# A gated attention and convolution block: the causal branch placed second, two more gate buffers, three rows of w_out and the post norm loaded during the last tiles

## The reference, cut to what matters

```python
h = rmsnorm(x, pre_norm_w[layer], NORM_EPS)                    # (2048, 1024)
proj = h @ w_in[layer]
(q, k, v, z_att, gb, gc, u, z_conv, g_att, g_conv) = jnp.split(proj, split_idx, axis=-1)
...
att = diff_attention(q, k, v, positions, lam)     # 4 heads, each the difference of two softmaxes
att = rmsnorm(att, subln_w[layer], SUBLN_EPS) * (1.0 - lambda_init)
att = att.reshape(b, s, ATT_WIDTH) * jax.nn.silu(z_att)
y_att = att @ w_att_out[layer]
cv = gb * short_conv(gc * u, conv_w[layer])
y_conv = (cv * jax.nn.silu(z_conv)) @ w_conv_out[layer]
m = (jax.nn.sigmoid(g_att + merge_bias[layer, 0]) * y_att
     + jax.nn.sigmoid(g_conv + merge_bias[layer, 1]) * y_conv)
x = x + rmsnorm(m @ w_out[layer], post_norm_w[layer], NORM_EPS)
```

## Time and profile before

| | us |
|---|---|
| median of 3 runs | 1817.24 (1812.0 to 1818.17) |
| profiled execution | 1817.06 |
| its span, first to last instruction | 1815.3 |
| PE busy in it | 1759.0 |
| DVE busy | 893.9 |
| ACT busy | 581.3 |

### The profile page before, as it was taken

How to read it: one execution, slowest core, us unless ns; L and a number is a source line. 1 busy time by engine, 2 the same in 40 slices (tenths; PEclk the granted TensorE clock), 3 DMA queues, 4 the chain that set the end, 5 groups by cost and what they waited for, 6 DMA issues and landing times.

```text
span 1815.3 us, 22423 instructions
## 1 busy us (share of the span) xinstructions
PE 1759.0 (97%) x8512; PEld 1467.5 (81%) x8512; DVE 893.9 (49%) x1903; ACT 581.3 (32%) x1039; POOL 89.2 (5%) x74
## 2 busy tenths in 40 slices
PE   6999999999999999999999999999999989999998
PEld 5878888888888888788887888888788768888887
DVE  5537225354433611267766666766666434424252
ACT  5422112121201111244444444444444333313231
POOL 0000000000000000111101112111001000000000
PEclk9999999999999999999999999999999999999999
DMA  6438536556503446976575678656756775453532
GB/s 220 141 135 329 193 133 209 186 186 196 174 24 113 153 120 158 285 219 192 186 196 184 202 218 271 212 177 209 237 167 171 234 280 172 116 184 107 179 105 75
DMA packets 149574, 328.90 MB, mean 181 GB/s; under 512 B 14801, under 2 KB 68049, under 8 KB 135889
## 3 DMA queue, kind: packets, MB, share of 16 engines
q1 hardware_dynamic: 149458, 327.37, 57.1%
HBM read 216.16 MB, written 111.16 MB: 180 GB/s over the span
## 4 chain that ended last, share of the span: by engine, by line
PE 86%; DMA 4%; ACT 3%; SPq 3%; DVE 2%; issue 2%; DVEq 0%; ACTq 0%
PE bank L935 19%; PE bank L936 19%; PE bank L937 19%; PE bank L1059 15%; PE bank L1021 5%; PE bank L993 3%; PE bank L994 3%; PE bank L1004 2%; SPq L667 2%; ACT e L1261 2%; DMA ring<-gate_s 1%; DMA w<-split_s 1%; PE bank L945 1%; DMA gate_s<-gate_st 1%; DVE at_lo L1609 1%
## 5 line engine op out<-in xcount | busy, mean ns | idle before, releaser
L935 PE MATMUL bank<-ht,w 128*128 128x512 f32 x896 | 349.4, 390 | 2.6 <-issue 2.6
L936 PE MATMUL bank<-ht,w 128*128 128x512 f32 x896 | 349.2, 390 | 0.0
L937 PE MATMUL bank<-ht,w 128*128 128x512 f32 x896 | 349.1, 390 | 0.0
L1059 PE MATMUL bank<-ht,w 128*128 128x512 f32 x912 | 238.8, 396 | 4.2 <-DMA w<-split_s 4.2
L935 PEld LDWEIGHTS bank<-ht,w 128*128 128x128 f32 x896 | 168.5, 188 | 38.0 <-ACT w L1173 3.0
L1059 PEld LDWEIGHTS bank<-ht,w 128*128 128x128 f32 x912 | 167.3, 190 | 37.0 <-DMA w<-split_s 4.8
L937 PEld LDWEIGHTS bank<-ht,w 128*128 128x128 f32 x896 | 168.7, 188 | 35.0
L936 PEld LDWEIGHTS bank<-ht,w 128*128 128x128 f32 x896 | 168.6, 188 | 35.0
L1573 DVE CUSTOM_DVE_ANT_0 e<-bank,zeros 128x512 f32<-128x512 f32 x192 | 125.0, 688 | 129.4 <-PE bank L994 128.9
L1261 ACT ACTIVATE e<-e,nbias 128x128 f32<-128x128 f32 (+15 forms) x128 | 152.9, 1198 | 74.8 <-DVE nbias L1582 74.6
L1059 PE MATMUL bank<-hx,w 128*128 128x512 f32 x576 | 157.2, 401 | 5.7 <-DMA w<-split_s 5.7
(11 more groups left out here) (140 smaller groups left out, 2497.0 us busy)
## 6 DMA issues: line engine op xcount, KB each, us to landing
w<-split_s SPq DMA_DIRECT2D x62, 1024.0 KB, 5.4
split_s<-piece SPq DMA_DIRECT2D x24, 1024.0 KB, 4.9
q_st<-qk_s SPq DMA_DIRECT2D x128, 128.0 KB, 5.6
gate_s<-gate_st SPq DMA_DIRECT2D x64, 256.0 KB, 6.0
ring<-gate_s SPq DMA_DIRECT2D x64, 256.0 KB, 3.4
raw<-in_w_in SPq DMA_DIRECT2D x28, 512.0 KB, 5.6
ht_s<-ht SPq DMA_DIRECT2D x3, 4096.0 KB, 27.5
qk_s<-stage SPq DMA_DIRECT2D x48, 192.0 KB
```

What stands on the lines that cost most here:

```text
L935: nc.tensor.matmul(out, left[0], right[0], start=start, stop=False)
L936: nc.tensor.matmul(out, left[0], right[1], start=False, stop=False)
L937: return nc.tensor.matmul(out, left[1], right[0], start=False, stop=stop)
L1059: mm = nc.tensor.matmul(bank[2 + u % 2][:], unit_weights(u)[:, term // 2, k, :], h_slot(bb, k)[:, term % 2, :], start=i == 0, stop=i == PE ...
```

## The change

The non-causal plan becomes the body of the `If` and the causal one that of the `Else`. Ring buffers 2 and 3 change places in SBUF with `wo_hi[0]`, `br[2]` and `br[3]`, and SP loads them at the end of `attend`, right behind 0 and 1; in the causal plan without a further wait. `wo_raw[4]`, `[5]`, `[7]` and `post_w` are loaded in round 61, behind `wa[3]`. The w_out rows are loaded and split in the order 4, 5, 7, 0, 1, 2, 3, 6, from m = 1 on. The other loads of the merge's first block (`wa[5]` to `wa[7]`, `wo_raw`) take new places between ring loads 5 to 15.

```diff
-WO_AT = ((), (), (0,), (1,), (2,), (3,), (4, 5), (6, 7))
+WO_AT = ((), (4,), (5,), (7,), (0,), (1,), (2,), (3, 6))
+WO_ORDER = (4, 5, 7, 0, 1, 2, 3, 6)
+WO_KEPT = 3
...
         for k in (4, 5, 6):
             late_br(k)
+        late_wo_hi(0)
+        late_br(2)
+        late_br(3)
         late_ring(2)
         late_ring(3)
-        late_br(2)
-        late_br(3)
-        late_wo_hi(0)
         late_wo_lo(0)
...
-            with eng.If(causal == 1):
+            with eng.If(causal == 0):
+                attend(Plan(False))
+            with eng.Else():
                 attend(Plan(True))
-            with eng.Else():
-                attend(Plan(False))
...
+            def load_wo(k):
+                i = WO_ORDER.index(k)
+                sp.dma_start(wo_raw[k][:], t["w_out"][k * P:(k + 1) * P, :]
+                             ).then_inc(wo_kept if i < WO_KEPT else wo_in[i - WO_KEPT], 16)
...
                                 load_branch(0, 2)
                                 load_branch(0, 3)
                                 load_wa(3)
+                                for k in WO_ORDER[:WO_KEPT]:
+                                    load_wo(k)
+                                sp.dma_start(post_w[:], t["post_norm_w"].to_broadcast([P, D])).then_inc(post_in, 16)
...
-                ring_load(0, 0)
-                ring_load(0, 1)
+                for i in range(2):
+                    ring_load(0, i)
+
+                if not plan.causal:
+                    sp.wait_ge(pv_done, PAIRS)
+                for i in range(2, 4):
+                    ring_load(0, i)
...
             sp.wait_ge(pv_done, PAIRS)
-            for i in range(2, RING):
-                ring_load(0, i)
+            ring_load(0, 4)
             sp.wait_ge(unit_done, UNITS)
...
             load_wa(4)
+            load_wa(5)
             for s_ in att_stored:
                 sp.wait_ge(s_, 16 * PAIRS // 2)
-            load_wo(0)
-            load_wo(1)
-            load_wa(5)
...
             for i in range(RING, 2 * KT):
                 ring_load(0, i)
-                if i == RING:
-                    load_wa(6)
-                    load_wo(2)
-                    load_wo(3)
-                elif i == RING + 1:
-                    load_wa(7)
-                elif i < RING + 6:
-                    load_wo(i - RING + 2)
-                elif i == RING + 7:
-                    sp.dma_start(post_w[:], t["post_norm_w"].to_broadcast([P, D])).then_inc(post_in, 16)
+                if i in (6, 9):
+                    load_wa(6 if i == 6 else 7)
+                elif i in (7, 8, 10, 12, 13):
+                    load_wo(WO_ORDER[WO_KEPT + (7, 8, 10, 12, 13).index(i)])
...
-                                pe.wait_ge(wo_lo_done, k + 1)
+                                pe.wait_ge(wo_lo_done, WO_ORDER.index(k) + 1)
```

More of the change, by code:

```diff
@@ L425, in build @@
         late_wa(3)
-        for k in (5, 6):
-            late_wo_hi(k)
-            late_wo_lo(k)
+        late_wo_hi(5)
+        late_wo_hi(6)
+        late_wo_lo(5)
+        late_wo_lo(6)
         late_wo_lo(7)
@@ L478, in build @@
         wa_in = [sem(f"wa_in{i}") for i in range(4)]
-        wo_in = [sem(f"wo_in{i}") for i in range(KT // 2)]
+        wo_kept, wo_in = sem("wo_kept"), [sem(f"wo_in{i}") for i in range(KT - WO_KEPT)]
         wo_hi_done, wo_lo_done = sem("wo_hi_done"), sem("wo_lo_done")
@@ L853, in _ @@
             sp.wait_ge(pv_done, PAIRS)
-            for i in range(2, RING):
-                ring_load(0, i)
+            ring_load(0, 4)
             sp.wait_ge(unit_done, UNITS)
-            def load_wo(k):
-                sp.dma_start(wo_raw[k][:], t["w_out"][k * P:(k + 1) * P, :]).then_inc(wo_in[k // 2], 16)
             load_wa(4)
+            load_wa(5)
             for s_ in att_stored:
                 sp.wait_ge(s_, 16 * PAIRS // 2)
-            load_wo(0)
-            load_wo(1)
-            load_wa(5)
             for s_ in gate_stored:
@@ L1336, in merge @@
                     for k in WO_AT[m] if n == 0 else ():
-                        act.wait_ge(wo_in[k // 2], 32)
+                        i = WO_ORDER.index(k)
+                        if i < WO_KEPT:
+                            act.wait_ge(wo_kept, 16 * WO_KEPT)
+                        else:
+                            act.wait_ge(wo_in[i - WO_KEPT], 16)
                         nc.scalar.activation(wo_hi[k][:], wo_raw[k][:], ACT.Copy).then_inc(wo_hi_done, 1)
@@ L1664, in _ @@
                     for k in WO_AT[m] if n == 0 else ():
-                        dve.wait_ge(wo_hi_done, k + 1)
+                        dve.wait_ge(wo_hi_done, WO_ORDER.index(k) + 1)
                         nc.vector.tensor_tensor(wo_lo[k][:], wo_raw[k][:], wo_hi[k][:].bitcast(F32), ALU.subtract
```

## The result

The changed kernel takes 1823.99 us (median of 6 runs, 1822.84 to 1829.85) against 1816.16 us for the kernel before in the same runs. The ratio is 1.0052, with a 95% interval of 1.0038 to 1.0065: slower, and by more than the 0.3% that the prediction takes for no change. The forecast was 1817.6 us and no change; the time lies half a microsecond above the wider of its two ranges, 1810.5 to 1823.5. The profiled execution of the changed kernel was its longest (1829.85 us, span 1828.0); that of a_again took 1823.3 us with a span of 1821.4. I read both, and say which.

The account below looks back on a forecast made before the run. The prediction took PE, busy 1759.0 of 1815.3 us, as the bound, with only its idle and low-clock stretches to change. 2.0 + 5.0 + 0.4 - 10.3 + 2.4 + 1.0 = +0.5 gave 1817.6 us; ranges 1813.5 to 1822 and, wider, 1810.5 to 1823.5.

Parts of the forecast that it names:

- The entry, +2.0 us: At the start of attention, engines now jump over the unused branch; SP's late gate store delays PE's value matmuls by 2.0 us.
- The loads ahead of `w`, +5.0 and +0.4: Before unit 62: 2048 KB of early loads delay `w` and PE by 5.0 us; lower clock behind the wait adds 0.4.
- The merge block, -10.3: First merge block, 192 `y` matmuls: PE's ring waits and the low-clock stretch go, winning 10.3 us.
- The tail, +2.4 and +1.0: Row matmuls after the last `y` matmul: PE waits 2.4 us for k = 3's split, then loses 1.0 at lower clock.
- neither of the two waits stays: First merge block: PE's waits of 2.13 and 4.71 us for gated ring buffers both vanish.
- Rival 3: Merge block: the ring chain stays the bound and one wait of 3 to 4 us remains, 1821 us; chance 0.1.
- Rival 2: Attention entry: SP's jump takes 9 us, delaying `q_st` and unit 4's `w`; the term becomes 8, time 1823.6; chance 0.17.

Follow-up runs that it names:

- a_again: The changed kernel itself, unaltered, run again in a later group for a second profile: 1823.3 us, ratio 1.0056 to the kernel before.
- d_split_rows_loads: Changed kernel with w_out rows split one m sooner, early loads behind the last `w`, causal branch first on PE and DVE only: 1810.11 us, 0.9978.
- c_rows_loads: Changed kernel with w_out rows split one m sooner and early loads behind the last `w`, causal branch still second on all engines: 1812.52 us, 0.9991.
- d_all_four: Changed kernel: rows split sooner, early loads behind `w`, PE taking rows 3, 6, 7 last at first, causal branch first on PE and DVE only: 1808.15 us, 0.9966.
- d_pe_order_rows_loads: Changed kernel: rows split sooner, early loads behind `w`, PE taking rows 3, 6, 7 last for two output tiles, causal branch second: 1812.45 us, 0.9990.
- e_before_split: Kernel before with only the branch placed by engine, causal first on PE and DVE, second on the others: 1813.08 us, 0.9979.
- b_branch_only: Kernel before with only the two branches exchanged, on all engines: 1815.82 us, 1.0001.
- a_loads_behind_w: Changed kernel with the three early `wo_raw` rows and `post_w` issued at the end of round 63, behind the last `w`: 1822.22 us, 1.0031.
- e_act_order: Changed kernel with ACT doing `m_hi` and the row split of m ahead of the second sigmoid of m + 1, first merge block: 1821.8 us, 1.0026.
- c_all_three: Changed kernel with causal branch first again, w_out rows split one m sooner and early loads behind the last `w`: 1811.66 us, 0.9989.

## Why the prediction was wrong

**The entry, +2.0 us: right at the place, too small at the end.** The forecast charged PE at the entry with the 3.58 us of its jump at the exit. The row says 7842 ns, and 4.64 us of it show. SP's jump was the other way round: between its branch at 761.1 and the gate store it issues at 763.89 lie 2.75 us, not the 5.6 read as its price at the exit, and ACT's eviction waited 2.70 us for that store, not 12. PE's value matmuls began at 770.25, for which 771.4 had been forecast, since the 3.77 us wait for unit 3's `w` took most of PE's delay, as the forecast said. Timelines of SP, ACT and PE of the changed kernel:

```profile
763.89 0.36 SPq L726 DMA_DIRECT2D gate_s<-gate_st  x1
...
766.80 0.60 ACT L1303 ACTIVATE gate_st<-bank 128x512 f32<-128x512 f32 x1 [2.70 <-DMA gate_s<-gate_st]
...
770.25 0.42 PE L1025 MATMUL bank<-at_hi,v_sl 128*128 128x256 f32 x2
```

At one and the same gate matmul just behind that wait the 9 profiles with the causal branch second on PE are later by 1.6 us on average than the 10 with it first (772.2 against 770.6). But the difference grows, to 4.7 us just ahead of unit 62 (1435.4 against 1430.7), and it grows in steps, at waits of PE for `w`. Near 960 us all of the 9 wait more than 1 us and only 2 of the 10; near 1113 us 6 of the 9 and none of the 10. The load that this second wait is for took 8.7 to 11.4 us from issue to landing in the 9 and 7.1 to 8.4 us in the 10. Why a load so far behind the entry is slower there is not settled. In medians PE's and DVE's place is worth 2.4 us (d_split_rows_loads against c_rows_loads), 4.3 (d_all_four against d_pe_order_rows_loads) and 4.0 (e_before_split against b_branch_only: 0.0022 of 1815).

Over all profiles PE's compare-and-branch took 88 ns where it fell through, 3344 to 5044 ns where it jumped at the exit and 7522 to 8259 ns where it jumped at the entry. "Advanced Engine Details and Errata", section Control Flow Timing, in the Trainium skill gives about 108 ns for a compare-and-branch; the 88 ns are near it, the jumps are not.

**The loads ahead of `w`, +5.0 and +0.4: right.** The wait went from 2.56 to 7.90 and 7.65 us, which is 5.1 to 5.3 us more, and moving the loads behind `w` gave 4.2 to 6.3 us where the tail was mended. Where it wasn't (a_loads_behind_w) the gain was 1 to 2 us in medians and some 4 by the ratios. Most of its y0 gain was lost ahead of unit 62 in that profile, in the spread just told; 1.2 us went in the block, to one ring wait of 0.87 us and what follows it.

**The merge block, -10.3: right in size.** It was 43.65 us, 10.1 less.

**The tail, +2.4 and +1.0: the step that failed.** Forecast was: "with 3.4 us for the load that is 5.45 us, the same as PE's". The 3.4 us are the median of all 64 ring loads. On the chain of this block in the changed kernel the first took 6.9 us and the next 5.4, with 1024 KB `wa` loads issued at 1466.37 and 1474.90 while they were under way, and then 4.0, 4.1, 4.0, 3.7 and 3.5. The chain's first two loads and three `m_lo`:

```profile
1463.47 6.94 DMA ring<-gate_s
...
1473.28 0.70 DVE m_lo L1670
...
1474.06 5.44 DMA ring<-gate_s
...
1480.79 0.70 DVE m_lo L1670
...
1486.84 0.70 DVE m_lo L1670
```

The rounds were 7.5 us, three of 6.0 to 6.1, 5.7 and 5.5, none as short as PE's 5.45, so DVE fell back. PE's `y` matmuls for m = 0 and 1 take 10.9 us from 1465.32, so they are done at 1476.2, and `m_lo` of m = 1 began 4.6 us later, at 1480.79. Those up to m = 6 take 38.2 us, to 1503.5, and its `m_lo` began 6.6 us later, at 1510.16. In e_act_order this lag is 2.4 to 2.6 us for every m. The four banks hid it as long as `y` matmuls ran, and this is why "neither of the two waits stays" came true; the lag was there at m = 6 and 7 all the same, and PE met it where it had no slack, at k = 2 (1.89 us) and k = 3 (3.81). The two waits make 5.7 us in place of 2.4, the 12 matmuls at the lower clock lose 2.4 us in place of 1.0, and the rest is smaller gaps. Together 8.5 us in place of 3.4. e_act_order takes the lag away and leaves the 2.41 us that DVE and ACT need for k = 3: the working of the 2.4 us was right, and its premise, that they keep step with PE, was not. Rival 3 had this mechanism but placed its wait among the `y` matmuls, and at 3 to 4 us.

**The sum.** With the measured terms it is 4.7 + 5.2 - 10.1 + 8.5 = +8.3 us, and the medians of the first comparison differ by 7.8. Against the forecast's +0.5 the tail is 5.1 us of the difference and the entry 2.7. The 4.7 us are a mean over profiles; a_again by itself has 7.8 - 10.1 + 8.5 = 6.2 us against the profile before, where the two spans differ by 6.1. Rival 2 named nearly the right time (1823.6) from another cause: the longer jump on SP did not occur. PE did wait 2.58 us for unit 4's `w` in the profile of the changed kernel, but 0.41 us in a_again, which was slower than the kernel before by as much.

What stays open: why the entry's delay grows between 770 and 1430 us, and how much of it is PE's jump and how much DVE's, since the two were moved together. Nor was the chain tried with ring loads of 3.4 us and ACT's old order: e_act_order shows that the order alone takes the lag away, not that the longer loads had no part in it. DVE's first maximum waits for PE's scores in the changed kernel, so its own jump doesn't show.

## What to carry to other kernels

When a chain through a DMA sets the pace, look at each engine in it for an instruction that is ready but queued behind one that waits for the transfer. Here one sigmoid ahead of `m_hi` made every round of the block depend on a load, and with it and two engines' jumps moved the old load order gave the same block of 43.65 us as the new one, without the 5 us ahead of unit 62 and the 8.5 at the tail. A lag hidden by buffers comes out at the first place without slack, so cost the end of a block with the pace of the slowest chain, by the load times of that very stretch and not by the median of all. And a large jump can be put, engine by engine, where that engine has slack.

## What the runs showed of the hardware

- A jump over the other branch body cost PE 3.34 to 5.04 us at the exit and 7.52 to 8.26 us at the entry of attention; in the changed kernel it was 7.84 us, with the DMA engines busy for 1.01 of the time by the window. The same instruction took 88 ns where it fell through. On SP it was the other way round: 2.75 us at the entry, and a gap of 5.63 us at the exit.
- The granted clock fell to 0.50 (1.2 GHz) around PE's longer waits, such as those of 7.90 and 3.81 us in the changed kernel. Around shorter ones it did in some profiles and not in others: with a wait of 2.41 us at the tail it fell in e_act_order (tail 13.38 us) and stayed at 1.00 in c_all_three (11.77), and the clock also stayed at 1.00 around a wait of 3.13 us for unit 62's `w` in d_pe_order_rows_loads.
